# The low parts of split weights, moved by 64 bytes

## The reference

```python
h = _rmsnorm(x, g_pre)
u = h @ w_in                                  # w_in: 2048 x 16192, each weight used once
...
y = gates[:, :, 0] * (branches[0] @ w_branch[0])
for n in range(1, N_BRANCH):
    y = y + gates[:, :, n] * (branches[n] @ w_branch[n])
return y @ w_out
```

## Time and profile before

| | |
|---|---|
| median of 3 runs | 3156.47 us (3155.7 to 3157.77) |
| span of the profiled execution | 3154.9 us, 52176 instructions |
| PE busy | 3134.1 us, 99% of the span |
| PEld busy | 2741.8 us, 87% |
| DVE, ACT busy | 2130.5 us (68%), 1733.0 us (55%) |
| DMA | 571.67 MB, mean 181 GB/s |

### The profile page before, as it was taken

One profiled execution on the slowest core, in us unless ns is written; L12 is line 12 of the kernel. 1 busy time (PEld: TensorE's weight loads), 2 busy tenths in 40 slices (PEclk: granted clock), 3 DMA queues, 4 the chain that ended last, 5 costly groups with the idle time before them and its releaser, 6 DMA issues.

```text
span 3154.9 us, 52176 instructions
## 1 busy us (share of the span) xinstructions
PE 3134.1 (99%) x18230; PEld 2741.8 (87%) x18230; DVE 2130.5 (68%) x2741; ACT 1733.0 (55%) x2291; POOL 0.2 (0%) x4
## 2 busy tenths in 40 slices
PE   9999999999999999999999999999999999999999
PEld 7888888888888788888888888888888888888888
DVE  7677575666667687766666555777776666655575
ACT  5685444444445556656555555645665656555563
POOL 0000000000000000000000000000000000000000
PEclk9999999999999999999999999999999999999999
DMA  7656655555556555565556655566556565665555
GB/s 230 194 168 200 198 187 166 183 177 172 181 167 208 178 168 163 156 198 173 174 171 192 184 181 182 181 198 186 158 157 202 170 179 167 192 189 180 178 185 175
DMA packets 569809, 571.67 MB, mean 181 GB/s; under 512 B 26352, under 2 KB 565488, under 8 KB 569712
## 3 DMA queue, kind: packets, MB, share of 16 engines
q1 hardware_dynamic: 569712, 570.42, 58.9%
HBM read 568.25 MB, written 2.10 MB: 181 GB/s over the span
## 4 chain that ended last, share of the span: by engine, by line
PE 97%; DVE 1%; ACT 1%; DMA 0%; SPq 0%; issue 0%; ACTq 0%; DVEq 0%
PE pg L537 91%; PE pa L771 1%; PE pa L788 1%; PE pa L537 1%; PE pa L778 1%; PE pa L747 1%; PE pa L789 1%; DVE hl L1276 0%; PE pa L704 0%; DMA raw<-w_o 0%; PE pa L878 0%; DMA raw<-w_in 0%; ACT hl L933 0%; SPq L456 0%; DVE uT L1357 0%
## 5 line engine op out<-in xcount | busy, mean ns | idle before, releaser
L537 PE MATMUL pg<-hT,hl 128*128 128x512 f32 x11456 | 2030.6, 337 | 1.1 <-DVE hl L1276 1.1
L537 PEld LDWEIGHTS pg<-hT,hl 128*128 128x128 f32 x11456 | 1750.9, 188 | 261.1 <-DVE hl L1276 4.2
L1276 DVE TENSOR_TENSOR hl<-raw,hl 128x1024 fp32r<-128x1024 f32 (+1 forms) x1071 | 1256.0, 1209 | 314.5 <-ACT hl L933 306.8
L933 ACT ACTIVATE hl<-raw 128x1024 fp32r<-128x1024 f32 (+1 forms) x1071 | 1084.0, 1044 | 313.1 <-PE pg L537 293.8
L537 PE MATMUL pg<-uT,hl 128*128 128x256 f32 (+1 forms) x3712 | 639.1, 333 | 15.9 <-DVE uT L1357 7.5
L537 PEld LDWEIGHTS pg<-uT,hl 128*128 128x128 f32 x3712 | 558.4, 190 | 92.2 <-issue 14.2
L941 ACT ACTIVATE corr<-pg 128x512 f32<-128x512 f32 x286 | 170.3, 596 | 843.0 <-PE pg L537 843.0
L537 PE MATMUL pg<-hl,hT 128*128 128x256 f32 (+1 forms) x1792 | 317.9, 336 | 0.0
L1283 DVE TENSOR_TENSOR work<-pg,corr 128x512 f32<-128x512 f32 (+1 forms) x154 | 105.8, 687 | 303.7 <-ACT corr L941 303.5
L537 PEld LDWEIGHTS pg<-hl,hT 128*128 128x128 f32 x1792 | 274.9, 188 | 40.7
L1283 DVE TENSOR_TENSOR gat<-pg,corr 128x512 f32 (+1 forms) x71 | 48.9, 689 | 139.4 <-ACT corr L941 139.4
(11 more groups left out here) (191 smaller groups left out, 1369.2 us busy)
## 6 DMA issues: line engine op xcount, KB each, us to landing
raw<-w_in SPq DMA_DIRECT2D x791, 512.0 KB, 4.7
raw<-w_br SPq DMA_DIRECT2D x96, 512.0 KB, 4.3
raw<-w_out SPq DMA_DIRECT2D x64, 512.0 KB, 4.7
raw<-w_rnn SPq DMA_DIRECT2D x32, 512.0 KB, 4.8
raw<-w_o SPq DMA_DIRECT2D x32, 512.0 KB, 5.0
raw<-w_att SPq DMA_DIRECT2D x16, 512.0 KB, 4.4
raw<-w_uq SPq DMA_DIRECT2D x16, 384.0 KB, 4.0
tab<-tabs SPq DMA_DIRECT2D x5, 896.0 KB, 7.2
```

The lines of the kernel that those rows point to most:

```text
L537: return nc.tensor.matmul(out, lhsT, rhs, start=start, stop=stop, skip_group_check=True)
L933: nc.scalar.activation(hl4[:, j % 2, 0, a:a + n], raw[:, bass.ds(j % 2 * UC + a, n)], ACT.Copy)\
L1276: tt(hl4[:, j % 2, 1, a:a + n], raw[:, bass.ds(j % 2 * UC + a, n)], hl4[:, j % 2, 0, a:a + n].bitcast(F32), ALU.subtract).then_inc(lo_done, 1)
```

## The change

The low parts are laid 16 float32 columns, that is 64 bytes, further. `hl` gets 64 columns more (256 bytes a partition), a slot is 4128 columns in place of 4096, and the low parts of a slot begin 2048 + 16 columns behind its high parts. The table `LO_SHIFT` has an entry for each slot and half, all 16. All views of `hl` are made by a function `part(j, e, h, a, n)` (slot, 0 high or 1 low, half, first column, count), or as lists of such slices. Instructions, their order, shapes and waits stay as they are; the tensors behind `hl` begin 256 bytes further.

```diff
+LO_SHIFT, LO_ROOM, SLOT = ((16, 16), (16, 16)), 32, 2 * UC + 32
...
-        hl = sb("hl", 4 * UC, F32R)
+        hl = sb("hl", 4 * UC + 2 * LO_ROOM, F32R)
...
-        hl4 = hl[:, :].rearrange("p (s h n) -> p s h n", s=2, h=2)
+        def part(j, e, h, a=0, n=UC // 2):
+            first = j % 2 * SLOT + e * UC + h * UC // 2 + (LO_SHIFT[j % 2][h] if e else 0) + a
+            return hl[:, first:first + n]
...
-                return [hl4[:, j % 2, h, :].rearrange("p (k n) -> p k n", n=n) if UC % n == 0 else
-                        hl4[:, j % 2, h, 0:UC // n * n].rearrange("p (k n) -> p k n", n=n) for h in range(2)]
+                return [[part(j, e, k * n // (UC // 2), k * n % (UC // 2), n) for k in range(UC // n)] for e in range(2)]
...
-                    lambda k, s: mm(pg3[:, b + s, :], wh[:, k - base, s * P:s * P + P], op[:, k, :], start and k == ks[0], False),
-                    lambda k, s: mm(pg3[:, b + s, S:], wl[:, k - base, s * P:s * P + P], op[:, k, 0:S], False,
+                    lambda k, s: mm(pg3[:, b + s, :], wh[k - base][:, s * P:s * P + P], op[:, k, :], start and k == ks[0], False),
+                    lambda k, s: mm(pg3[:, b + s, S:], wl[k - base][:, s * P:s * P + P], op[:, k, 0:S], False,
-                    lambda k, s: mm(pg3[:, b + s, :], op[:, k, s * P:s * P + P], both[:, k - base], start and k == ks[0], False),
-                    lambda k, s: mm(pg3[:, b + s, S:], op[:, k, S + s * P:S + s * P + P], hiw[:, k - base], False,
+                    lambda k, s: mm(pg3[:, b + s, :], op[:, k, s * P:s * P + P], both[k - base], start and k == ks[0], False),
+                    lambda k, s: mm(pg3[:, b + s, S:], op[:, k, S + s * P:S + s * P + P], hiw[k - base], False,
-                return [hl4[:, j % 2, h, :].rearrange("p (s n) -> p s n", s=2)[:, :, 0:n] for h in range(2)]
+                return [[part(j, e, h, 0, n) for h in range(2)] for e in range(2)]
-                return hl4[:, j % 2, :, :].rearrange("p h (k n) -> p k h n", n=n)
+                views = []
+                for k in range(UC // n):
+                    h, a = k * n // (UC // 2), k * n % (UC // 2)
+                    apart = UC + LO_SHIFT[j % 2][h]
+                    first, a = j % 2 * SLOT, h * UC // 2 + a
+                    views.append(hl[:, first:first + 2 * apart].rearrange("p (e n) -> p e n", e=2)[:, :, a:a + n])
+                return views
...
-                    wh, wl = (w.rearrange("p h (k n) -> p h k n", n=P) for w in apart_view(j, 512))
+                    wh, wl = ([[w[h][:, k * P:k * P + P] for k in range(4)] for h in range(2)] for w in apart_view(j, 512))
...
-                wh, wl = (w.rearrange("p h (k n) -> p h k n", n=384) for w in apart_view(0, 768))
+                wh, wl = apart_view(0, 768)
-                        w = [x[:, k // 2, k % 2, a:a + P] for x in (wh, wl)]
+                        w = [x[k // 2][:, k % 2 * 384 + a:k % 2 * 384 + a + P] for x in (wh, wl)]
...
-                    nc.scalar.activation(hl4[:, j % 2, 0, a:a + n], raw[:, bass.ds(j % 2 * UC + a, n)], ACT.Copy)\
+                    nc.scalar.activation(part(j, 0, h, 0, n), raw[:, bass.ds(j % 2 * UC + a, n)], ACT.Copy)\
...
-                    tt(hl4[:, j % 2, 1, a:a + n], raw[:, bass.ds(j % 2 * UC + a, n)],
-                       hl4[:, j % 2, 0, a:a + n].bitcast(F32), ALU.subtract).then_inc(lo_done, 1)
+                    tt(part(j, 1, h, 0, n), raw[:, bass.ds(j % 2 * UC + a, n)], part(j, 0, h, 0, n).bitcast(F32),
+                       ALU.subtract).then_inc(lo_done, 1)
```

More of the change, by code:

```diff
@@ L628, in unit @@
                         if form == "r":
-                            ins = feature_major(b, subs, wh[:, h], wl[:, h], op, ks, begin, end, base + 4 * h, side)
+                            ins = feature_major(b, subs, wh[h], wl[h], op, ks, begin, end, base + 4 * h, side)
                         elif form == "t":
@@ L658, in last_unit_by_bank @@
                     for k in range(8, 16):
-                        mm(pg3[:, 2 + s, :], wh[:, k - 8, col], op[:, k, :], False, False)
-                        ins = mm(pg3[:, 2 + s, S:], wl[:, k - 8, col], op[:, k, 0:S], False, k == 15)
+                        mm(pg3[:, 2 + s, :], wh[k - 8][:, col], op[:, k, :], False, False)
+                        ins = mm(pg3[:, 2 + s, S:], wl[k - 8][:, col], op[:, k, 0:S], False, k == 15)
                     if s == 0:
@@ L812, in keys_and_values @@
                     for k in range(2):
-                        w = [x[:, k, S * e:S * e + P] for x in (wh, wl)]
+                        w = [x[k][:, S * e:S * e + P] for x in (wh, wl)]
                         ins = three_terms(pg3[:, b, e * S:e * S + S], *w, u3[:, 12 + k, 0:S], u3[:, 12 + k, S:], k == 0, k == 1)
                 ins.then_inc(a_part, 1)
-                vh, vl = (w.rearrange("p k (e n) -> p k e n", e=2)[:, :, :, P:S] for w in (wh, wl))
+                vh, vl = ([x.rearrange("p (e n) -> p e n", e=2)[:, :, P:S] for x in w] for w in (wh, wl))
                 for t in range(2):
@@ L819, in keys_and_values @@
                         xh, xl = (u3[:, 12 + k, a + t * P:a + t * P + P] for a in (0, S))
-                        ins = three_terms(pg3[:, b + 1, t * S:t * S + S], xh, xl, vh[:, k], vl[:, k], k == 0, k == 1)
+                        ins = three_terms(pg3[:, b + 1, t * S:t * S + S], xh, xl, vh[k], vl[k], k == 0, k == 1)
                 ins.then_inc(half_done, 2)
@@ L1074, in _ @@
                     act.wait_ge(first_landed, 16)
-                    nc.scalar.activation(hl4[:, 0, 0, 0:512], raw[:, 0:512], ACT.Copy).then_inc(first_hi, 1)
+                    nc.scalar.activation(part(0, 0, 0, 0, 512), raw[:, 0:512], ACT.Copy).then_inc(first_hi, 1)
                 elif n == 1:
                     act.wait_ge(raw_landed[0][0], 16)
-                    nc.scalar.activation(hl4[:, 0, 0, 512:1024], raw[:, 512:1024], ACT.Copy).then_inc(hi_done, 1)
+                    nc.scalar.activation(part(0, 0, 0, 512, 512), raw[:, 512:1024], ACT.Copy).then_inc(hi_done, 1)
                     hi(U_RX, 0, (1,))
@@ L1480, in _ @@
                     dve.wait_ge(first_hi, 1)
-                    tt(hl4[:, 0, 1, 0:512], raw[:, 0:512], hl4[:, 0, 0, 0:512].bitcast(F32), ALU.subtract).then_inc(first_lo, 1)
+                    tt(part(0, 1, 0, 0, 512), raw[:, 0:512], part(0, 0, 0, 0, 512).bitcast(F32), ALU.subtract).then_inc(first_lo, 1)
                 elif n == 1:
                     dve.wait_ge(hi_done, 1)
-                    tt(hl4[:, 0, 1, 512:1024], raw[:, 512:1024], hl4[:, 0, 0, 512:1024].bitcast(F32), ALU.subtract)\
+                    tt(part(0, 1, 0, 512, 512), raw[:, 512:1024], part(0, 0, 0, 512, 512).bitcast(F32), ALU.subtract)\
                         .then_inc(lo_done, 1)
```

## The result

The changed kernel takes 3162.72 us (median of 15 runs) where the kernel before takes 3156.78 (3155.7 to 3157.86) in the same session: ratio 1.0018, 95% interval 1.0011 to 1.0026. One of the fifteen took 12273.2 us and stays out of the ratio; the median of the other fourteen is 3162.60. The kernel is slower by 5.9 us, which is real, and lies within the 0.2% that the forecast counted as no change, with 0.4 us to spare. The spans of the profiled executions, 3161.1 and 3154.9 us, differ by 6.2.

What follows compares the result with a forecast made beforehand. TensorE's matmul count times pace was taken to bound the kernel; all terms were priced 0, summing to 0 on the 3154.9 us span, and with 1.6 us around it the forecast was 3156.5 us, range 3055 to 3182.

Steps and rivals of the forecast that it cites:

- the likeliest case: No change in the kernel's time, 3150 to 3163 us around 3156.5; chance 0.48.
- The signs named for it: 1040 matmuls, give or take two, in 180 us; 188 ns per load; 1221 and 1053 ns on VectorE and ScalarE.
- What bounds the kernel: TensorE's number of matmuls times their pace; its matmuls wait for other engines only 17.1 us in all.
- The cost of 13 ns per load: Each matmul's weight load on TensorE adds 13.2 ns beyond its columns at full clock, nothing at half clock.
- VectorE's and ScalarE's writes: VectorE writing shifted low parts, ScalarE's high copies unmoved: 0, bounded by 3 us of VectorE time either way.
- Everything behind `hl` lies 256 bytes further: Other tiles keep their place within 128 bytes, and no instruction, wait, queue or transfer is added: 0.
- Slot 1's move by 128 bytes: Second slot of the split weights moves 128 bytes; included in the VectorE and ScalarE write step, priced 0.
- 64 bytes in itself slows neither read: Moved low parts as weights in 7,520 narrow matmuls: taken as 0, between 99 us less and 99 us more.
- R2: Slower rival: shifted low weights touch five 128-byte blocks instead of four, 25 us more (3181), 3256 if read twice; chance 0.20.
- Low parts as moving operand: 896 wide matmuls in token-major units stream low parts 64 bytes off: 0, at worst 3 us more, or the same won.
- R1: Faster rival: TensorE's two reads meet by address, so low weight loads cost less; 3057, or 3107 if half freed; chance 0.32.
- R3: Rival: `hl` not at a multiple of 128, so the change doesn't do what it says; 3156.5; chance 0.02 within no change.

Runs made afterwards that it cites:

- e8: Changed kernel edited so high and low parts alike lie 64 bytes beyond a multiple of 128, their distance kept; 3192.57 us, 1.0110 of the kernel before.
- e3: Changed kernel with split weights put back as before and only what lies behind `hl` 256 bytes further; 3157.18 us, 1.0000 of the kernel before.
- e1: Changed kernel with the 64-byte shift taken back but the room kept (slot 1 128 bytes further, tensors behind 256); 3185.31 us, 1.0089 of the kernel before.
- e7: Changed kernel with all low parts shifted by 96 bytes, all else at its place modulo 512; 3183.63 us, 1.0082 of the kernel before.
- e11: Changed kernel with only the token-major units' low parts put back at a multiple of 128, places kept modulo 512; 3160.11 us, 1.0010 of the kernel before.
- e12: Changed kernel with only the token-major units' low parts shifted 64 bytes, all others at a multiple of 128; 3161.26 us, 1.0014 of the kernel before.
- e5: Changed kernel with all low parts shifted by 128 bytes, all else at its place modulo 512; 3164.11 us, 1.0022 of the kernel before.
- e6: Changed kernel with all low parts shifted by 32 bytes, all else at its place modulo 512; 3167.28 us, 1.0032 of the kernel before.
- e2: Changed kernel with the 64-byte shift kept and everything else back at its place modulo 512; 3163.61 us, 1.0018 of the kernel before.

## Why the prediction was right, and where its reasons failed

**The time, the range and the side were right:** 3156.5 was forecast, 3162.7 came, inside the likeliest case's own range of 3150 to 3163 and within 0.2%. The signs named for it came too: 1039 matmuls in the stretch, 188, 1221 and 1054 ns. That it came so near is in part luck, as the step that failed shows.

**What bounds the kernel: right.** TensorE's waits came to 17.8 us against 17.1, and the rest is pace. The cost of 13 ns per load is there after the change too, and nil at half clock in the changed kernel and in e8. That the other engines' reads and writes have no part in it holds in e8's stretch, as shown above. The sentence of the Trainium skill that the forecast weighed (TensorE: Matmul & The Clock Gate, "Step-by-step: what each phase is for": two independent read ports, no bandwidth taken by the next weights) agrees no better with the traces after it: in e8 a matmul takes 180.00 / 1020 = 176.5 ns against 173.2, where only addresses differ.

**VectorE's and ScalarE's writes, priced 0: right**, 1221 and 1054 ns.

**"Everything behind `hl` lies 256 bytes further ... 0": right** for that step (e3, ratio 1.0000). Slot 1's move by 128 bytes, priced 0 with VectorE's writes, was not free by rule: with the room alone, e1 is 28 us slower.

**"64 bytes in itself slows neither read ... I take 0": the step that failed.** It came from loads and matmuls at half rate (in `work`, 256 columns take 220 ns from start to start, where one column a cycle would be 107), where a load has room to hide, as the forecast itself said of R2. At full rate the shift changes wide and narrow matmuls in turn alike (394 to 392, 277 to 280 ns). The 0 came out for this order only because both patterns sum to 32 cycles per matmul, and that is luck: by the same reasoning 96 bytes would cost nothing, and e7 is 26 us slower. The same step in the pair order costs 2.5 us.

**Low parts as moving operand, 0 with 3 us as the bound: mis-sized.** Token-major units take 3.4 us more, just beyond the bound, and e11 shows that putting their low parts back takes this away. It isn't one more block of 128 bytes per matmul, since in e12 the same moved columns cost 1.1 us.

**R1 had the right premise and the wrong end.** The cost does depend on address, and the wide matmuls did get shorter, but by 2 ns, and the narrow ones longer by 3. Nothing tried got below 32 cycles in the order in turn. **R2 had the right direction,** but its blocks of 128 bytes fall with e5, e6 and e7: by blocks e5 would cost nothing and e6 as much as e7. **R3** falls with e2: the shift does something.

**What stays open.** The runs show that each matmul with its load loses time beyond its columns at full rate, in repeating patterns that depend on addresses and on what went before. That the two reads of TensorE meet is the likeliest reading, and no run looks at the reads themselves. The runs don't show the rule by which a given pair of addresses stalls, how a pattern outlasts the attention's matmuls in between, nor why the narrow ones in runs come down to 18 cycles in e8 while matmuls in turn, wide and narrow together, never get below 32.

## What to carry to other kernels

Where a kernel is bound by back-to-back matmuls with a weight load each, the place of its tiles in a partition can be worth 1% (0 to +35 us here), and waits and busy shares don't warn of it (PE is 99% busy in e1 and e8 too): count the matmuls in a stretch without idle time, or lay the same matmuls of two traces side by side. Any new tile or padding ahead of the operands can move that 1%, so a change that shifts addresses by accident should be timed against one with the same shift and nothing else. A result found in one order of matmuls (in turn) doesn't hold in another (pairs, runs, operands swapped), and not even for the same unit behind another neighbour.

## What the runs showed of the hardware that was not expected

A shift of 128 bytes in one slot and of 256 in what lies behind, which leaves every operand's place within 128 bytes alone, costs 28 us (e1), and 64 bytes in both weight parts 35 us (e8), while the 256 bytes by themselves cost nothing (e3). Weights and activations at the same addresses lose 32 cycles a matmul in e3 and 40 in e1, by what the other slot holds. Units whose addresses stand as before modulo 512 run 0.21 us slower in 64 matmuls when token-major units ahead of them have other addresses (e12). VectorE's and ScalarE's traffic has no part in it: in e8 a matmul loses the same 52 or 28 cycles with both idle as with both busy.
